# Rotary rows of the four query tiles gathered into one tile by transfers inside SBUF and rotated once, in a hybrid encoder layer

## The reference, cut to what matters

```python
def partial_rope(t, pos):
    ...
    tr = t[..., :ROT_DIM].astype(jnp.float32)
    t1, t2 = tr[..., :half], tr[..., half:]
    rot = jnp.concatenate([t1 * cos - t2 * sin, t2 * cos + t1 * sin], axis=-1).astype(t.dtype)
    return jnp.concatenate([rot, t[..., ROT_DIM:]], axis=-1)
...
    proj = h @ w_in
    ...
    q = partial_rope(b_q.reshape(bsz, s, N_Q_HEADS, HEAD_DIM), pos)
    k = partial_rope(b_k.reshape(bsz, s, N_KV_HEADS, HEAD_DIM), pos)
    yb = window_attention_with_sink(q, k, v, attn_sink) * jax.nn.silu(b_z)
```

## Time and profile before

| | |
|---|---|
| median of 3 runs | 926.77 us (925.99 to 927.73) |
| the profiled execution | 925.96 us |
| its span, first to last instruction | 924.1 us |
| PE busy | 907.8 us, 98% of the span |
| DVE, ACT, POOL busy | 657.1, 439.2, 453.4 us |
| mean granted TensorE clock | 0.996 |

### The profile page before, as it was taken

The page is one execution under the profiler, slowest core; times in us unless marked ns, Lnnn a source line. Parts: engine busy times, 40 slices in busy tenths (PEclk is TensorE's granted clock), DMA queues, the critical chain, the costliest instruction groups (busy, mean ns, idle before and its releaser), DMA issues.

```text
span 924.1 us, 12763 instructions
## 1 busy us (share of the span) xinstructions
PE 907.8 (98%) x4376; PEld 763.3 (83%) x4376; DVE 657.1 (71%) x1060; ACT 439.2 (48%) x849; POOL 453.4 (49%) x303
## 2 busy tenths in 40 slices
PE   9999999999999999999999999999999999999995
PEld 8788788888888888888888888888888888888784
DVE  5689976565656566656576178888797358899887
ACT  7624464444444466544463434343444544445341
POOL 3546844444444444444446744444443636668452
PEclk9999999999999999999999999999999999999998
DMA  7243846252525242525255322222222974750333
GB/s 287 96 116 83 228 144 210 90 171 91 170 91 169 96 128 102 193 91 171 108 174 174 116 80 80 79 78 82 80 69 68 333 262 143 258 181 0 142 110 137
DMA packets 82336, 126.56 MB, mean 137 GB/s; under 512 B 7136, under 2 KB 40544, under 8 KB 82272
## 3 DMA queue, kind: packets, MB, share of 16 engines
q1 hardware_dynamic: 81952, 125.61, 41.2%
q10 hardware_dynamic: 320, 0.13, 0.1%
HBM read 92.56 MB, written 33.55 MB: 136 GB/s over the span
## 4 chain that ended last, share of the span: by engine, by line
PE 81%; DVE 8%; ACT 3%; DMA 3%; POOL 2%; issue 2%; SPq 1%; DVEq 0%; ACTq 0%
PE pm L866 17%; PE pm L864 17%; PE pm L865 17%; PE pm L1162 3%; PE pm L1163 3%; PE pm L1161 3%; PE pv L999 2%; PE sa L987 2%; PE sa L1163 2%; PE sa L1162 2%; PE sa L1161 2%; PE pv L1078 2%; PE sa L1058 1%; DVE area L2158 1%; DVE area L2135 1%
## 5 line engine op out<-in xcount | busy, mean ns | idle before, releaser
L766 POOL TENSOR_TENSOR ring<-spots,ring 128x512 fp32r<-128x512 f32 x234 | 340.9, 1460 | 389.9 <-ACT ring L1207 377.9
L864 PE MATMUL pm<-hc,ring 128*128 128x512 f32 x784 | 308.6, 394 | 0.0
L866 PE MATMUL pm<-hc,ring 128*128 128x512 f32 x784 | 305.8, 390 | 0.0
L865 PE MATMUL pm<-hc,ring 128*128 128x512 f32 x784 | 305.5, 390 | 0.0
L1207 ACT ACTIVATE ring<-spots 128x512 fp32r<-128x512 f32 x234 | 146.2, 628 | 268.6 <-PE pm L866 177.5
L866 PEld LDWEIGHTS pm<-hc,ring 128*128 128x128 f32 x784 | 147.2, 188 | 31.2
L864 PEld LDWEIGHTS pm<-hc,ring 128*128 128x128 f32 x784 | 147.3, 188 | 29.3 <-issue 0.6
L865 PEld LDWEIGHTS pm<-hc,ring 128*128 128x128 f32 x784 | 147.4, 188 | 28.9
L1161 PE MATMUL pm<-hc,ring 128*128 128x512 f32 x128 | 49.9, 390 | 0.0
L1162 PE MATMUL pm<-hc,ring 128*128 128x512 f32 x128 | 49.8, 389 | 0.0
L1163 PE MATMUL pm<-hc,ring 128*128 128x512 f32 x128 | 49.8, 389 | 0.0
(11 more groups left out here) (248 smaller groups left out, 1664.5 us busy)
## 6 DMA issues: line engine op xcount, KB each, us to landing
spots<-in_w SPq DMA_DIRECT2D x116, 256.0 KB, 3.2
raw_d<-area SPq DMA_DIRECT2D x72, 256.0 KB, 2.0
area<-raw_d SPq DMA_DIRECT2D x24, 512.0 KB, 4.4
area<-in_x SPq DMA_DIRECT2D x16, 512.0 KB, 4.2
spots<-in_wup SPq DMA_DIRECT2D x24, 256.0 KB, 4.5
spots<-in_wout SPq DMA_DIRECT2D x20, 256.0 KB, 3.7
q_d<-area_r SPq DMA_DIRECT2D x16, 256.0 KB, 4.3
area<-raw_d SPq DMA_DIRECT2D x16, 256.0 KB, 3.6
```

The source lines that it names most:

```text
L766: nc.gpsimd.tensor_tensor(ring_part(n, 1), operand(n), ring_part(n, 0).bitcast(F32), ALU.subtract).then_inc(lo_made, 1)
L864: pe.matmul(bank, hi, moving_hi(k), start=(k == 0), stop=False)
L865: pe.matmul(bank, hi, moving_lo(k), start=False, stop=False)
L866: mm = pe.matmul(bank, lo, moving_hi(k), start=False, stop=(k == HC - 1))
```

## The change

The query tiles are no longer rotated whole. ACT copies each query tile from PSUM to SBUF (`copy_query`), splits the copy at once (`high_query` on ACT, `query_low_part` on POOL), and SP stores the 48 plain rows of every head (`store_query`, four transfers of 48 partitions). The 16 rotary rows of each of the eight heads are moved by SP into one tile of 128 partitions (`gather`, two transfers of 16 partitions for each tile, inside SBUF). That tile is rotated once by the four DVE operations (`swap_gathered`, `rotate(1)`) with tables that SP loads a second time in 16 pieces of 16 partitions (`load_gathered_tables`), split, and stored in 16 transfers of 16 partitions (`store_gathered`). The copies and the key rotation use the storage of T4's split form as scratch, so ACT's `high_of_combination(T4)` now waits for the queries' low parts and for the gathers. `q_d` is laid out by head with whole rows of 1024 tokens, so the stores write rows of 4 KB and each `load_block` reads runs of 512 bytes. The load of the first block takes all four heads of a group at once, and ACT's own transfers (`last_queries`) are gone. PE's waits for a free PSUM tile are now on `query_copied` in place of `cos_made`. Some semaphores of later stages are merged into one, with the same waits.

```diff
-        rope_high_at = [f32r(at, SEQ) for at in (QHI0, QHI0 + SEQ, QHI0, QHI0 + SEQ, SWAP0)]
-        rope_low_at = [f32r(at, SEQ) for at in ROTATED]
+        flat = hc_f32[:, T4, :, :, :].rearrange("p t k s -> p (t k s)")
+        t4_quarter = [flat[:, n * SEQ:(n + 1) * SEQ] for n in range(4)]
+        rotated = (t4_quarter[0], f32(GATHER0, SEQ))
+        swap = (t4_quarter[1], f32(TURNED0, SEQ))
+        rope_high_at = (f32r(KHI0, SEQ), f32r(TURNED0, SEQ))
+        rope_low_at = (f32r(KHI0 + SEQ, SEQ), f32r(GATHER0, SEQ))
+        query_raw = [t4_quarter[2 + c % 2] for c in range(GROUP)]
...
...
+            def gather(c):
+                sp.wait_ge(query_copied, c + 1)
                 for g in range(2):
...
+                    at = g * HEAD + c * ROT
+                    sp.dma_start(f32(GATHER0, SEQ)[at:at + ROT, :],
+                                 query_raw[c][g * HEAD:g * HEAD + ROT, :]).then_inc(gathered[c % 2], 16)
+            def store_query(c):
+                sp.wait_ge(query_lo, c + 1)
+                for part, src in enumerate((query_high[c], query_low[c])):
+                    for g in range(2):
+                        to = ((1 - g) if part else g) * HEAD
+                        sp.dma_start(q_d[GROUP * g + c, to + ROT:to + HEAD, :],
+                                     src[g * HEAD + ROT:(g + 1) * HEAD, :].bitcast(F32)).then_inc(query_stored[c], 16)
+            def store_gathered():
+                sp.wait_ge(rope_lo, 2)
+                for part, src in enumerate((rope_high_at[1], rope_low_at[1])):
+                    for g in range(2):
+                        to = ((1 - g) if part else g) * HEAD
+                        for c in range(GROUP):
+                            at = g * HEAD + c * ROT
+                            sp.dma_start(q_d[GROUP * g + c, to:to + ROT, :],
+                                         src[at:at + ROT, :].bitcast(F32)).then_inc(rope_stored, 16)
+            def store_keys():
+                high, low = rope_high_at[0].bitcast(F32), rope_low_at[0].bitcast(F32)
+                sp.wait_ge(rope_lo, 1)
                 for g in range(2):
                     own, other = slice(g * HEAD, (g + 1) * HEAD), slice((1 - g) * HEAD, (2 - g) * HEAD)
...
+                    sp.dma_start(kh_d[own, g, :], high[own, :]).then_inc(rope_stored, 16)
+                    sp.dma_start(kh_d[other, g, :], high[own, :]).then_inc(rope_stored, 16)
+                    sp.dma_start(kl_d[own, g, :], low[own, :]).then_inc(rope_stored, 16)
+            def load_gathered_tables():
+                sp.wait_ge(roped, 1)
+                for dst, src in ((cosb, cos), (sinb, sin)):
+                    for n in range(HEADS):
+                        sp.dma_start(dst[n * ROT:(n + 1) * ROT, :], src[0:ROT, :]).then_inc(rope_landed, 16)
...
             sp.dma_start(sinb, sin).then_inc(rope_landed, 16)
+            gather(0)
             for j in range(4):
                 load_spot(j, 2)
-            store_rope(0)
+            gather(1)
+            store_query(0)
+            store_keys()
+            store_query(1)
+            load_gathered_tables()
             load_spot(A11, 3)
             load_spot(A12, 3)
-            store_rope(1)
+            gather(2)
+            store_query(2)
             load_spot(A21, 3)
             load_spot(A22, 3)
-            store_rope(2)
+            gather(3)
+            store_query(3)
             def store_raw(p, side, half, made):
...
                     sp.wait_ge(zero_stored, 16 * 4)
-                    sp.dma_start(q_stack_f32[:, :, 0:GROUP - 1, :], q_d[0][:, :, 0:GROUP - 1, :]).then_inc(q_landed, 16)
                 else:
                     sp.wait_ge(scored, 8 * i)
-                    sp.dma_start(q_stack_f32, q_d[i]).then_inc(q_landed, 16)
+                sp.dma_start(q_stack_f32, q_d[:, :, i * P:(i + 1) * P].rearrange("(g h) p q -> p g h q", g=2)
+                             ).then_inc(q_landed, 16)
                 sp.dma_start(kwin_hi_f32, kh_d[:, :, first:first + WIN]).then_inc(kh_landed, 16)
                 sp.dma_start(kwin_lo_f32, kl_d[:, :, first:first + WIN]).then_inc(kl_landed, 16)
...
-                        store_query_part(4, 0)
+                        store_gathered()
                         load_block(0)
-                        store_query_part(4, 1)
                     if 0 <= gr < ATT_GROUPS - 1 and gr % 2 == 1:
...
             low_part(7)
+            low_part(8)
+            query_low_part(0)
+            low_part(9)
             rope_low(0)
-            low_part(8)
-            low_part(9)
-            rope_low(1)
-            for n in range(10, 15):
-                low_part(n)
-            rope_low(2)
+            query_low_part(1)
+            low_part(10)
+            low_part(11)
+            query_low_part(2)
+            low_part(12)
+            low_part(13)
+            query_low_part(3)
+            low_part(14)
             for j in (0, 2):
                 low_of_combination(T1, j)
             low_part(15)
-            low_part(16)
-            rope_low(3)
-            for n in range(17, 20):
+            rope_low(1)
+            for n in range(16, 20):
                 low_part(n)
-            rope_low(4)
             for n in range(20, NS + 3):
                 low_part(n)
...
                     t = 2 * p + side
-                    if t >= 3:
-                        before = [c for c, _ in ROPES].index(t - 3)
-                        pe.wait_ge(cos_made, before + 1)
+                    if t == 3:
+                        pe.wait_ge(cos_made, 1)
...
-                    pe.wait_ge(cos_made, 4)
-                else:
-                    pe.wait_ge(cos_made, 5)
+                    pe.wait_ge(query_copied, 3)
+                else:
+                    pe.wait_ge(query_copied, 4)
...
                     wait_slot(act, 2, "A21")
+                elif idx == T4:
+                    act.wait_ge(rope_lo, 1)
+                    act.wait_ge(query_lo, GROUP)
+                    for j in range(2):
+                        act.wait_ge(gathered[j], 64)
                 for j in range(HC):
-                    act.wait_ge(sum_made[idx], j + 1)
+                    act.wait_ge(sum_made[idx], sums_before(idx) + j + 1)
                     nc.scalar.activation(hc[:, idx, 0, j, :], f32(SUM_AT[idx] + j * HALF, HALF),
...
+                    act.wait_ge(comb_dve, HC)
+                nc.scalar.activation(rope_high_at[j], rotated[j], ACT.Copy).then_inc(rope_hi, 1)
+            def copy_query(c):
+                wait_slot(act, (c + 1) // 2, ("A12", "A22")[(c + 1) % 2])
+                if c >= 2:
+                    act.wait_ge(query_lo, c - 1)
+                    act.wait_ge(gathered[c % 2], 32)
+                nc.scalar.copy(query_raw[c], tile_bank(c + 1)).then_inc(query_copied, 1)
+            def high_query(c):
+                if c == 0:
                     act.wait_ge(sum_made[T2], HC)
-                    act.wait_ge(h_lo_pool, h_lo_count(2 * KC - 1, h_lo_pool))
-                nc.scalar.activation(rope_high_at[j], rotated(j), ACT.Copy).then_inc(rope_hi, 1)
+                elif c == 2:
+                    act.wait_ge(rope_stored, 16 * 6)
+                else:
+                    wait_query_stored(act, c // 2)
+                act.wait_ge(query_copied, c + 1)
+                nc.scalar.activation(query_high[c], query_raw[c], ACT.Copy).then_inc(query_hi, 1)
             high_part(6)
             high_part(7)
+            copy_query(0)
             act.wait_ge(ssq_made, NB - 1)
             high_of_combination(T3)
-            rope_high(0)
             high_part(8)
+            high_query(0)
             high_of_combination(T2)
...
             high_part(10)
-            high_of_combination(T4)
             high_part(11)
+            copy_query(2)
+            high_query(2)
             high_part(12)
             high_part(13)
+            copy_query(3)
+            high_query(3)
+            high_of_combination(T4)
             high_part(14)
-            rope_high(2)
             high_of_combination(T1)
...
...
+            def swap_keys():
+                dve.wait_ge(slot_done, TILE_SLOTS[0])
+                nc.vector.stream_shuffle(swap[0], tile_bank(0), SWAP_ROWS).then_inc(swapped, 1)
                 dve.wait_ge(rope_landed, 32)
...
+                nc.vector.tensor_tensor(rotated[0], tile_bank(0), cosb, ALU.mult).then_inc(cos_made, 1)
+            def swap_gathered():
+                for j in range(2):
+                    dve.wait_ge(gathered[j], 64)
+                nc.vector.stream_shuffle(swap[1], rotated[1], SWAP_GATHERED).then_inc(swapped, 1)
+                dve.wait_ge(swapped, 2)
+                dve.wait_ge(rope_landed, 16 * (2 + 2 * HEADS))
+                nc.vector.tensor_tensor(rotated[1], rotated[1], cosb, ALU.mult).then_inc(cos_made, 1)
             def rotate(j):
                 dve.wait_ge(swapped, j + 1)
...
```

(20 more changed lines are left out.)

138 lines of the change are left out of this document (47 added, 91 removed).

## The result

The changed kernel takes **940.38 us** at the median of three runs (938.51, 940.38, 941.5), beside 926.38 (925.06 to 927.73) for the kernel before on the same chip: 14.0 us more, ratio 1.0146, 95% interval 1.013 to 1.0163. A fourth run took 1539.49 us in the slow state, at a mean granted clock of 0.556, and is left out (with it the median would be 940.94). The profiled execution took 938.51 us with a span of 936.4, so its span is 12.3 us longer than that of before (924.1). The forecast of 939.7 us and its range hold; the distribution of the time inside does not, as the rows show.

The account below looks back on a forecast made before the run. The prediction took PE, busy in 98% of the span, as the bound. To 925.96 us it added 11.7 for the later first scores and 2.0 for the clock, giving 939.7 us, range 930 to 951.

Parts of the forecast that it names:

- the case named as likeliest: Rival A: PE stalls a little at P6, P7, P4 and long before the first scores; 933 to 945, chance 0.60.
- Step 1: SP ahead of pair 3: keys ready at 62.9, tables 10.1 us until 81.5, weights still in time for P1 at 87.76.
- the text's own mark for a mis-sized step 1: Sign of error: P1 of pair 3 late by more than 1 us.
- Step 2: The last gather, behind ACT's copy of query tile 3: issued until 88.2, landed about 90.3, POOL's low part at 90.4.
- Step 3: Queues behind the last gather on ACT, POOL and DVE delay P6, P7, P4 and P5: PE slips by 6.3 us.
- Step 4: First block's loads wait behind 16 stores of 10.1 us: scores start at 126.7, 11.7 us later, PE idle 6.9.
- Step 5: Clock after the gap before the first scores: PE drops to 1.2 GHz, 2.0 us lost, ends 0 and 4.
- I price this at nothing: DVE's removed operations and later blocks' queries read in 512-byte runs were each taken to change the time by nothing.
- B: Narrow transfers on SP's queue back up at 0.94 us each, 9.9 us more: 949.6; chance 0.20.
- C: SP's queue is quick, 0.49 us each; POOL and DVE collide less, clock stays up: 931.2; chance 0.14.
- D: Everything added is hidden and the old 1.53 us wait before the first scores goes too: 924.4; chance 0.02.
- E: The change doesn't matter: SP's idle queue and PE's ready time hide it, old wait kept: 926.0; chance 0.04.

Follow-up runs that it names:

- the test on the kernel before: The kernel before with sixteen idle transfers of 16 partitions added on SP's queue ahead of pair 3's weights: 932.81 us, ratio 1.0059.
- both orders first: The changed kernel with slot 16's low part ahead of the gathered tile on POOL and T4's low parts ahead of the rotation on DVE: 943.38 us, ratio 1.0174.
- tables early: The changed kernel with the 16 table loads moved ahead of the key stores in SP's program: 934.56 us, ratio 1.0087.
- the reordered version: The changed kernel with several orders on SP, ACT and POOL changed at once, and the gathered high half stored early: 930.09 us, ratio 1.0034.

## Why the prediction was right, point by point

- **Total.** 939.7 forecast, 940.38 measured (938.51 in the profiled execution). Of the case named as likeliest, the small stalls at P6, P7 and P4 and the later stores came; the long stall before the first scores did not. That the number is so close is in part luck. The forecast was made of 6.3 us of slip, 6.9 of idle time at the scores less the old 1.53, and 2.0 of clock; the trace has 10.5 of gaps and 3.4 of clock less the old 1.53. The sums are alike because PE's own chain, which I had taken too short, ended within some 1.0 us of the chain of transfers.
- **Step 1** was mis-sized by one term. The keys were 4.2 us late: 3.4 of this is POOL's low part (2.43 taken, 5.85 measured), the rest a later start. The tables were 1.8 us cheaper than taken, and P1 was 2.0 us late (89.78 against 87.76) instead of on time: the text's own mark for a mis-sized step 1.
- **Step 2** was right in its mechanism. The last gather was issued until 91.70 (88.2 forecast), and this lateness comes from step 1. Its two transfers took 3.3 and 3.6 us to land instead of 2.8 (the median of all eight is 2.6), so T4's highs started at 94.61 instead of 90.4.
- **Step 3** named all the waits, their order and their engines. The term "T4's low parts, 4.71" failed: 7.84 with POOL at work. Slot 14's 1.98 was 1.27. P6, P7 and P4 start at 98.82, 105.49 and 112.15 where 95.2, 101.1 and 105.9 were forecast. Of P4's 6.2 us, 4.0 are the rotation, which ended at 104.2 instead of 100.2, and 3.1 the low parts; 1.0 goes off because the forecast had P4 wait for slot 16, 1.0 us behind these low parts. The text's sum is also off in the small: 101.3 + 2.43 is 103.7 and not 103.9, and 105.9 + 10.1 in step 4 is 116.0 and not 115.8, which cancel.
- **Step 4** had nearly the right end for a chain with wrong parts. The 16 stores began 4.3 us later than forecast (110.24 against 105.9, slot 16 being late), took 7.36 us instead of 10.1 (0.46 each, below my lower end of 0.49) and landed sooner; the block's loads went from 119.33, and their landing allows the scores at about 126.5, against 126.7 forecast. The idle 6.9 us did not come, because PE itself had lost 14.0 us by then and was ready at 127.44 and not at 119.8.
- **Step 5** had about the right price and the wrong place: 1.7 us twice, behind gaps of 3.31 and 3.66 us, instead of 2.0 once behind 6.9. Its reading of the earlier trace rows is half supported: the row at the program's end shows the clock of 0.53, but the one of 1 to 5 us has a granted clock of 1.00 beside its 19 matmuls, which the text passes over. "The gap of 1.53 us left no such mark" holds here up to 2.21, but see below.
- **"I price this at nothing"** (DVE's saved work, the 512-byte runs) held: DVE's 12.3 us less bought nothing, and the layout alone has a ratio of 0.9997.
- **Rivals.** B (0.94 each) fell: bursts of sixteen cost 0.46 and 0.52 in the change, 0.70 in the test on the kernel before. C had the queue's price about right (0.49), but not that POOL and DVE would collide less, nor that the clock would stay up. D (nearly nothing, with the Trainium skill's DMA: Bandwidth & Descriptors, issuing engines) fell too: one issue of 0.46 us is small beside its landing of 2.0, but sixteen in a row held the weights up for 8.3 us. E fell with the ratio of 1.0146.

The 14.0 us of the medians divide as follows. 8.3 go with the tables on the queue, and 5.8 of these are their place alone. The order of SP, ACT and POOL as a whole, with all tables loaded, recovers 10.3 (940.38 to 930.09). The last 3.0 to 3.7 (the kernel before took 927.07 beside that version and 926.38 beside the change) stayed in every version. In the best of them the traces show DVE and POOL holding each other up, one fall of the clock and, in one, ACT's queue behind the rotated tile; no version was free of all of these, so how the rest divides stays open.

## What to carry to other kernels

Count the issue slots before you count saved operations: 12 operations less on an engine with slack bought nothing, and 16 narrow loads ahead of the weights on the same queue cost 8.3 us of 926. When a step is gathered into one, its single late result stands in the in-order program of every engine that touches it, and each of those programs has to be looked at: here curing POOL's order exposed DVE's, and curing that exposed ACT's. Take the duration of a VectorE or GpSimd operation from a row in which the other is as busy as it will be. And before you call an order better or worse, subtract what the clock took: it can hide a change of 2 us or feign one of 5.

## What the runs showed of the hardware that was not expected

- **POOL shut out by a dense run of DVE, or the reverse.** The same POOL operation took 5.84 or 5.85 us beside DVE operations of 0.62 each in seven traces of the change and its versions, and 2.82 or 2.83 us in the other four, in which DVE's took 1.17 each. In all eleven it started 1.31 or 1.32 us after the first of DVE's four, so the start times do not tell which way it goes, and what decides is open. The Trainium skill (SBUF — State Buffer, on the two separate sides) calls the shared ports an exclusive lock, where the other fully blocks; the 2.27 us from DVE's last operation to POOL's end agree. POOL was not let in at any of the five changes of operation on DVE that followed its start, so its wait went beyond a single instruction.
- **The clock falls behind short gaps, and not always.** Between 84 and 135 us of these traces a granted clock near half, the lower level of 1.2 GHz, followed each of the 19 gaps of 2.26 us and more. It also followed one of 1.82 (both orders first) and one of 2.08 (tables early), and did not follow one of 1.83, one of 2.21 or any shorter one. Of the 21 falls, 17 took 1.5 to 1.7 us of PE's time and four took 2.6 to 3.0; the longest gap, 4.28, had a short one. The mean clock of the change's runs varied too, 0.994 in the profiled one and 0.988 in the one of 941.5 us. The Trainium skill (TensorE: Matmul & The Clock Gate, Part 1) says that the count of slow matmuls at a kernel's start varies from run to run of one kernel; whether the spread of 3 us here, wider than that of the reordered version (1.2), is of that kind no run shows.
- **A narrow transfer's issue** cost 0.46 us in a burst of stores, 0.52 for the tables and 0.70 from DRAM to DRAM, for the same 64 KB.
